# Byte offsets of the split weight slots in a decoder layer with a PEER expert network

## The chip, the cores and the metric

The kernel runs on one core of a Trainium2 chip. The metric is the device time of one execution in microseconds; the number compared is the median of several runs. One execution was also taken by the hardware profiler, and every row quoted here is from that one.

## What is computed

One layer on 256 tokens of 2048 float32 values. A projection feeds two mixers (a gated depthwise convolution with a layer norm, and a short gated convolution); their outputs go through a second projection and a layer norm. Then comes a PEER block: each token picks, for 8 heads, 16 of 16384 experts.

```
h  = x @ w_in + b_in
a  = silu(layer_norm(causal_conv31(a_val * sigmoid(a_gate))))
s  = sc_b * causal_conv3(sc_c * sc_h)
x1 = layer_norm(alpha * x + concat(a, s) @ w_out + b_out)
q  = x1 @ w_q;  scores against sub_keys;  top 16 of the sums -> experts, softmax g
act  = gelu(x1 . peer_u[experts]);  coef = act * g
x2 = layer_norm(alpha * x1 + sum(coef * peer_v[experts]))
```

## The kernel before, in words

The kernel does not gather the experts' rows of `peer_u`: it multiplies all of `peer_u` with x1, applies gelu, multiplies with a mostly zero matrix of gates, and multiplies the result with `peer_v`. For half of the columns of the second token block (`picked`) it gathers rows of `peer_v` instead, with POOL's indirect DMAs, and VectorE adds them up.

Float32 products are made from split numbers. Each number is written as hi + lo, both in the format float32r, and a product is three matmuls: hi by hi, hi by lo, lo by hi. The weights stream in as 656 units of 128 x 1024 float32 (512 KB), numbered `u`: 80 of `w_in`, 32 of `w_out`, 32 of `w_q`, 256 of `peer_u` ("up") and 256 of `peer_v` ("down"). For each unit:

- SP's queue loads it into a slot of `raw` (4 slots; in the down stage also 3 of `raw_late`), once the split of the unit that was there is done (`load`, L467).
- ACT copies it into `w_hi[u % 4]` (function `hi`, L627), once TensorE has used that slot's unit of four before (`used`).
- DVE subtracts, `w_lo[u % 4] = raw - w_hi` (function `lo`, L843); for the units of `w_q` and the first 36 of `peer_u` POOL does it instead (L571).
- PE waits for `lo_done` and runs its matmuls.

There are two kinds of unit on PE. For `w_in`, `w_q` and `peer_u` (368 units, function `stationary_unit`, L1411 to L1413) the weights are the stationary operand, 128 columns at a time, and the split x (`xt_hi`, `xt_lo`, 128 x 16 x 256) is the moving one, 256 columns: 24 matmuls a unit, 16 of them on `w_hi` and 8 on `w_lo`. For `w_out` (`out_units`, L1460 to L1462, split activations `mix_hi`, `mix_lo`) and `peer_v` (`down`, L1587 to L1589, split coefficients `c0` to `c4`) the roles are exchanged: 128 columns of activations or coefficients are stationary and 512 columns of weights move. The last four units of all do not go to `w_hi` and `w_lo` but to eight buffers of their own, `tail_hi0` to `tail_lo3`, and are read twice, once for each block of 128 tokens.

Between the up units, 32 batches of 8 short matmuls (L1553) build the gates from one-hot tables `oh1` (bfloat16) and `oh2g` (float16), 256 moving columns each.

SBUF is laid out by the order of the calls of `sb`, with some regions stacked on one another (`down0`, `down1`, `down2`, `early`, `route`). Each tensor takes its bytes per partition, rounded up to a multiple of 32. So the distance between two tensors follows from the sizes between them: from the end of `w_lo3` to the first of the split coefficients lie `stats` (192 bytes), `mv` (32), `rstd` (32) and `neg_mean` (32), together 288. All of `xt_hi`, `xt_lo`, `mix_hi`, `mix_lo`, the coefficient sets, `oh1`, `oh2g`, `raw_late`, `rows` and the `tail` buffers follow it at multiples of 128 bytes from each other; each slot of `w_hi` and `w_lo` starts at a multiple of 128 bytes from `raw`. The second family therefore stands 288 - 256 = 32 bytes off the first, counted modulo 128 (and modulo 64). The rows within a tensor step by 512, 1024 or 2048 bytes and change nothing in this.

```
mm(dst, hi_w[:, sl], xt_hi[:, kk, :], start=st, stop=False)
mm(dst, hi_w[:, sl], xt_lo[:, kk, :], start=False, stop=False)
i = mm(dst, lo_w[:, sl], xt_hi[:, kk, :], start=False, stop=en)
```

Of the kernel before, what the change touches and what calls it, by code (L numbers as in the profile page):

```python
# [5 lines left out]
P = 128  # L6
# [4 lines left out]
HALF = KT // 2  # L11
# [38 lines left out]
SPLIT = 4  # L50
# [116 lines left out]
def build(nc, x_t, x_nat, w_in, w_out, w_q, u_w, v_w, params, sub_keys, b_out, ln1_g, ln1_b, ln2_g, ln2_b, out):  # L167
    f32 = mybir.dt.float32
    f32r = mybir.dt.float32r
# [9 lines left out]
    with ctx:  # L179
        def sb(name, shape, dt, where=ctx):  # L180
            return where.enter_context(nc.sbuf_tensor(name, shape, dt))
# [2 lines left out]
            return ctx.enter_context(nc.semaphore(name))  # L184

        raw = sb("raw", [P, RAW, HALF * P], f32)
        w_hi = [sb(f"w_hi{i}", [P, HALF * P], f32r) for i in range(SPLIT)]
        w_lo = [sb(f"w_lo{i}", [P, HALF * P], f32r) for i in range(SPLIT)]
        stats = sb("stats", [P, TB, NCH, 6], f32)
        mv = sb("mv", [P, TB, 2], f32)  # L190
        rstd = sb("rstd", [P, TB, 1], f32)
        neg_mean = sb("neg_mean", [P, TB, 1], f32)

        def coefs(name, where):
            return [sb(f"{name}_{part}", [P, GROUP, T], f32r, where) for part in ("hi", "lo")]
# [1492 lines left out]
```

## Time and profile before

| | |
|---|---|
| median of 3 runs | 1747.68 us (1747.27 to 1749.12) |
| span of the profiled execution, first to last instruction | 1745.8 us |
| PE busy | 1713.3 us, 98% of the span |
| DVE busy | 1407.6 us, 81% |
| ACT busy | 854.0 us, 49% |
| POOL busy | 540.4 us, 31% |
| HBM traffic | 327 GB/s over the span |

The profiled execution's own time is given as its span; the median lies 1.9 us above it, which is work around the first and the last instruction. Busy time of PE counts a stretch as busy as long as some matmul is in flight; the matmuls overlap, so it does not tell whether they follow each other as closely as they could. That is read from the distance between the starts of neighbouring matmuls.

### The profile page before, as it was taken

To read this page: it belongs to the slowest core of one execution; us is meant where nothing else is said; L and a number is where in the kernel's file an instruction comes from. 1 tells how busy PE (TensorE), PEld (TensorE's weight loads), DVE (VectorE), ACT (ScalarE), POOL (GpSimd) and SP (SyncE) were. 2 spreads that over 40 slices of the span, in tenths; PEclk is the share of its full clock that TensorE was granted. 3 is DMA by queue.
4 is the path that set the end of the run, shared out by engine and by line. 5 is a ranking of instruction groups with operands and counts; after the bars stand their busy time and mean duration, and the time that the engine had idled before them with its cause. 6 is when DMAs were issued, how large, how long until landed. Compare 5 with 4: busy or idle time off the path is not lost.

```text
span 1745.8 us, 31461 instructions
## 1 busy us (share of the span) xinstructions
PE 1713.3 (98%) x11910; PEld 1578.1 (90%) x11910; DVE 1407.6 (81%) x1998; ACT 854.0 (49%) x1084; POOL 540.4 (31%) x342
## 2 busy tenths in 40 slices
PE   8999999899999999999999999999999999999997
PEld 8999987799999999999999999998788777878776
DVE  7999997678967677777777777556899898999997
ACT  5544436344544444444444444445555555555544
POOL 0000000288881000000000000004787777777731
PEclk9999999999999999999999999999999999999999
DMA  7787787777777777777677777899899999999994
GB/s 267 267 276 267 234 260 249 273 237 235 250 249 252 238 236 244 247 235 239 237 241 239 236 244 243 282 355 332 314 400 400 399 401 389 400 399 395 369 398 133
DMA packets 173728, 504.52 MB, mean 289 GB/s; under 512 B 19408, under 2 KB 35920, under 8 KB 172624
## 3 DMA queue, kind: packets, MB, share of 16 engines
q1 hardware_dynamic: 134000, 427.08, 70.0%
q0 software_dynamic: 22528, 67.19, 10.0%
q10 hardware_dynamic: 17120, 9.35, 1.8%
q8 instruction: 29, 0.48, 0.1%
q14 instruction: 51, 0.42, 0.1%
HBM read 490.98 MB, written 79.69 MB: 327 GB/s over the span
## 4 chain that ended last, share of the span: by engine, by line
PE 78%; DMA 6%; DVE 6%; issue 5%; POOL 3%; ACT 1%; DVEq 1%; SPq 0%; POOLq 0%; ACTq 0%
PE psum L1411 18%; PE psum L1413 18%; PE psum L1412 18%; PE psum L1587 6%; PE psum L1589 6%; PE psum L1588 6%; POOL sp_coef L588 2%; DVE w_lo L843 2%; DMA raw<-in_v_w_dram 2%; PE psum L1553 2%; DMA raw_late<-in_v_w_dram 1%; PE psum L1460 1%; PE psum L1462 1%; PE psum L1461 1%; DVE psum L1312 1%
## 5 line engine op out<-in xcount | busy, mean ns | idle before, releaser
L627 ACT ACTIVATE w_hi<-raw 128x1024 fp32r<-128x1024 f32 x547 | 578.9, 1060 | 682.1 <-PE psum L1413 487.1
L1411 PE MATMUL psum<-xt_hi,w_hi 128*128 128x256 f32 x2944 | 827.2, 281 | 5.3 <-DVE xt_lo L857 3.1
L1412 PE MATMUL psum<-xt_lo,w_hi 128*128 128x256 f32 x2944 | 822.6, 279 | 0.0
L1413 PE MATMUL psum<-xt_hi,w_lo 128*128 128x256 f32 x2944 | 822.4, 279 | 0.0
L843 DVE TENSOR_TENSOR w_lo<-raw,w_hi 128x1024 fp32r<-128x1024 f32 x479 | 581.8, 1222 | 221.5 <-ACT w_hi L627 219.7
L1411 PEld LDWEIGHTS psum<-xt_hi,w_hi 128*128 128x128 f32 x2944 | 554.3, 188 | 6.6 <-issue 6.0
L1412 PEld LDWEIGHTS psum<-xt_lo,w_hi 128*128 128x128 f32 x2944 | 554.3, 188 | 0.0
L1413 PEld LDWEIGHTS psum<-xt_hi,w_lo 128*128 128x128 f32 x2944 | 554.1, 188 | 0.0
L582 POOL DMA_INDIRECT rows<-v_rows,sp_idx x96 | 130.9, 1364 | 709.7 <-issue 674.9
L1587 PE MATMUL psum<-w_hi,c_hi 128*128 128x512 f32 x752 | 299.7, 399 | 8.9 <-DVE w_lo L843 8.7
L1589 PE MATMUL psum<-w_hi,c_lo 128*128 128x512 f32 x752 | 298.2, 396 | 0.0
L1588 PE MATMUL psum<-w_lo,c_hi 128*128 128x512 f32 x752 | 297.9, 396 | 0.0
L571 POOL TENSOR_TENSOR w_lo<-raw,w_hi 128x1024 fp32r<-128x1024 f32 x68 | 164.7, 2427 | 364.3 <-ACT w_hi L627 364.2
L588 POOL DMA_INDIRECT sp_coef<-hid_spill,sp_idx x128 | 193.0, 1508 | 55.2 <-issue 45.9
L1587 PEld LDWEIGHTS psum<-w_hi,c_hi 128*128 128x128 f32 x752 | 141.7, 188 | 49.5 <-DVE w_lo L843 15.4
L1589 PEld LDWEIGHTS psum<-w_hi,c_lo 128*128 128x128 f32 x752 | 141.6, 188 | 34.3
L1588 PEld LDWEIGHTS psum<-w_lo,c_hi 128*128 128x128 f32 x752 | 141.7, 188 | 33.3
L627 ACT ACTIVATE w_hi<-raw_late 128x1024 fp32r<-128x1024 f32 x105 | 111.3, 1060 | 103.2 <-PE psum L1589 75.0
L843 DVE TENSOR_TENSOR w_lo<-raw_late,w_hi 128x1024 fp32r<-128x1024 f32 x105 | 126.6, 1221 | 8.4 <-ACT w_hi L627 8.4
L1312 DVE SCALAR_TENSOR_TENSOR psum<-rows,sp_coef,psum 128x1024 f32<-128x1024 f32 x95 | 121.8, 1282 | 3.2 <-DMA rows<-v_rows,sp_idx 2.3
L882 DVE SCALAR_TENSOR_TENSOR cacc<-apad,prm,cacc x232 | 101.3, 480 | 0.0
L1293 DVE TENSOR_TENSOR c_lo<-hid,c_hi 128x1024 fp32r<-128x1024 f32 x32 | 39.2, 1224 | 22.9 <-ACT c_hi L776 22.8
(164 smaller groups left out, 1131.8 us busy)
## 6 DMA issues: line engine op xcount, KB each, us to landing
raw<-in_u_w_dram SPq DMA_DIRECT2D x256, 512.0 KB, 4.2
raw<-in_v_w_dram SPq DMA_DIRECT2D x148, 512.0 KB, 8.7
v_rows<-in_v_w_dram SPq DMA_DIRECT2D x128, 512.0 KB, 5.2
raw_late<-in_v_w_dram SPq DMA_DIRECT2D x108, 512.0 KB, 8.9
raw<-in_w_in_dram SPq DMA_DIRECT2D x80, 512.0 KB, 4.3
raw<-in_w_out_dram SPq DMA_DIRECT2D x32, 512.0 KB, 4.5
raw<-in_w_q_dram SPq DMA_DIRECT2D x32, 512.0 KB, 4.5
hid_spill<-hid ACTq DMA_DIRECT2D x7, 1024.0 KB, 15.4
```

The lines of the kernel that those rows point to most:

```text
L571: nc.gpsimd.tensor_tensor(w_lo[s][:, :], raw[:, s, :], w_hi[s][:, :].bitcast(f32), ALU.subtract).then_inc(lo_done[s], SPLIT)
L582: nc.gpsimd.indirect_dma_start(rows[k % ROWS][:, :], None, v_rows, bass.IndirectOffsetOnAxis(sp_idx[:, 1, k:k + 1], 0)).then_inc(rows_in[k ...
L588: nc.gpsimd.indirect_dma_start(sp_coef[:, k:k + 1], None, hid_dram, bass.IndirectOffsetOnAxis(sp_idx[:, 0, k:k + 1], 0)).then_inc(act_in[k ...
L627: nc.scalar.activation(parts_of(slot_u)[0][:, :], raw_of(slot_u), ACT.Copy).then_inc(hi_done, 1)
L843: tt(lo_w[:, :], raw_of(slot_u), hi_w[:, :].bitcast(f32), ALU.subtract).then_inc(lo_done[slot_u % SPLIT], SPLIT)
L1312: i = stt(picked[:, :], rows[k % ROWS][:, :], sp_coef[:, k:k + 1], picked[:, :], ALU.mult, ALU.add)
L1411: mm(dst, hi_w[:, sl], xt_hi[:, kk, :], start=st, stop=False)
L1412: mm(dst, hi_w[:, sl], xt_lo[:, kk, :], start=False, stop=False)
L1413: i = mm(dst, lo_w[:, sl], xt_hi[:, kk, :], start=False, stop=en)
L1587: mm(v_bank(j, b), c1, w1, start=st, stop=False)
L1588: mm(v_bank(j, b), c1, w2, start=False, stop=False)
L1589: i = mm(v_bank(j, b), c2, w1, start=False, stop=en)
```

## The change

The four slots of `w_hi` become slices of one tensor that is 6 elements longer, and start 0, 2, 4 and 6 elements (0, 8, 16, 24 bytes) behind a multiple of 4096 bytes. The four slots of `w_lo` become slices of one tensor that is 24 elements longer, and start 4, 8, 16 and 24 elements (16, 32, 64, 96 bytes) behind it. A tensor `place_pad` of 96 bytes that nothing uses is put in front of the coefficients. The number and order of the instructions on every engine, their shapes, waits and DMAs stay as they were; only addresses differ.

```
-        w_hi = [sb(f"w_hi{i}", [P, HALF * P], f32r) for i in range(SPLIT)]
-        w_lo = [sb(f"w_lo{i}", [P, HALF * P], f32r) for i in range(SPLIT)]
+        def placed(name, steps):
+
+            whole = sb(name, [P, SPLIT * HALF * P + steps[-1]], f32r)
+            return [whole[:, i * HALF * P + step:(i + 1) * HALF * P + step] for i, step in enumerate(steps)]
+
+        w_hi = placed("w_hi", [0, 2, 4, 6])
+        w_lo = placed("w_lo", [4, 8, 16, 24])
         stats = sb("stats", [P, TB, NCH, 6], f32)
         mv = sb("mv", [P, TB, 2], f32)
         rstd = sb("rstd", [P, TB, 1], f32)
         neg_mean = sb("neg_mean", [P, TB, 1], f32)
+        sb("place_pad", [P, 24], f32)
```

Rounded up to 32, the new `w_hi` is 32 bytes longer than the four old ones, the new `w_lo` 96 bytes, and the pad adds 96: from `w_hi0` on, the second family moves by 224 bytes, and its offset becomes 32 + 224 = 256, that is 0 modulo 128. Against it the weight slots stand so:

| slot | 0 | 1 | 2 | 3 |
|---|---|---|---|---|
| `w_hi`, bytes | 0 | 8 | 16 | 24 |
| `w_lo`, bytes | 48 | 64 | 96 | 128 |

(`w_lo` has 32 bytes more than its steps because it starts 32 bytes later behind the longer `w_hi`.) The `tail` buffers keep an offset of 0 against the coefficients, as before. `raw` stays where it was; `raw_late`, `rows` and `row_late`, which DMAs fill, move with the second family.

## Rows read from the trace of the kernel before

**Rows 1.** The page: busy time by engine, and the 40 slices.
```profile
PE 1713.3 (98%) x11910; PEld 1578.1 (90%) x11910; DVE 1407.6 (81%) x1998; ACT 854.0 (49%) x1084; POOL 540.4 (31%) x342
PEclk9999999999999999999999999999999999999999
```

**Rows 2.** Stages by window: PE, PEld, DVE, ACT, POOL busy, clock, DMA share, GB/s.
```profile
0.00:1184.00 1184.00, 1170.52 (x9607) 1145.95 (x9608) 905.23 (x1535) 552.93 (x788) 166.44 (x80) 1.00 0.75 253
1184.00:1716.00 532.00, 523.13 (x2220) 416.39 (x2220) 482.94 (x431) 292.94 (x283) 366.34 (x256) 1.00 1.00 381
```

**Rows 3.** Timeline of PE in the up stage, first and 148th of a run.
```profile
1109.98 0.28 PE L1411 MATMUL psum<-xt_hi,w_hi 128*128 128x256 f32 x1
...
1127.13 0.28 PE L1411 MATMUL psum<-xt_hi,w_hi 128*128 128x256 f32 x1
```

**Rows 4.** Timeline of PE in the down stage, first and 73rd of a run.
```profile
1561.67 0.40 PE L1587 MATMUL psum<-w_hi,c_hi 128*128 128x512 f32 x1
...
1578.47 0.40 PE L1587 MATMUL psum<-w_hi,c_hi 128*128 128x512 f32 x1
```

**Rows 5.** Timeline of PE, first pass over the tail units; 12 matmuls lie between the rows.
```profile
1719.20 0.39 PE L1588 MATMUL psum<-tail_lo,c_hi 128*128 128x512 f32 x1
...
1721.92 0.39 PE L1588 MATMUL psum<-tail_lo,c_hi 128*128 128x512 f32 x1
```

**Rows 6.** Timeline of PE, second pass: the first tail matmul, the sixth, the eighth, the last.
```profile
1730.02 0.39 PE L1587 MATMUL psum<-tail_hi,c_hi 128*128 128x512 f32 x1
...
1731.17 0.39 PE L1589 MATMUL psum<-tail_hi,c_lo 128*128 128x512 f32 x1
...
1731.63 0.39 PE L1588 MATMUL psum<-tail_lo,c_hi 128*128 128x512 f32 x1
...
1735.25 0.39 PE L1589 MATMUL psum<-tail_hi,c_lo 128*128 128x512 f32 x1
```

**Rows 7.** Timeline of PE, one batch of gates: start, time, and x8 merged.
```profile
700.67 1.08 PE L1553 MATMUL psum<-oh2g,oh 128*128 128x256 f16 x8
```

**Rows 8.** PE's groups by line and shape: count, busy us, mean ns, idle before.
```profile
L1411 PE MATMUL psum<-xt_hi,w_hi 128*128 128x256 f32 x2944 | 827.2, 281 | 5.3 <-DVE xt_lo L857 3.1 <-issue 2.3
L1587 PE MATMUL psum<-w_hi,c_hi 128*128 128x512 f32 x752 | 299.7, 399 | 8.9 <-DVE w_lo L843 8.7
L1460 PE MATMUL psum<-w_hi,mix_hi 128*128 128x512 f32 x128 | 51.0, 399 | 1.9 <-DVE mix_lo L997 1.1 <-DVE lnt L1024 0.8
```

**Rows 9.** DMA in 40 slices of 1200 to 1700 us, and its sum.
```profile
GB/s 401 234 285 277 403 398 402 400 400 400 399 398 403 399 399 399 403 400 400 399 378 383 401 399 401 402 400 402 390 403 402 380 401 392 343 350 408 410 408 400
DMA packets 58255, 193.15 MB, mean 386 GB/s; under 512 B 10119, under 2 KB 10123, under 8 KB 58238
```

**Rows 10.** DVE's and ACT's splits by line: min/median/max ns.
```profile
L843 DVE TENSOR_TENSOR w_lo<-raw,w_hi x479: 1202/1224/1298, 5.2 to 1715.4; 128x1024 fp32r<-128x1024 f32 x160
L843 DVE TENSOR_TENSOR w_lo<-raw_late,w_hi x105: 1205/1217/1273, 1195.4 to 1712.0; 128x1024 fp32r<-128x1024 f32 x105
L627 ACT ACTIVATE w_hi<-raw x547: 1041/1062/1071, 4.0 to 1713.2; 128x1024 fp32r<-128x1024 f32 x183
L627 ACT ACTIVATE tail_hi<-raw_late x3: 1041/1043/1062, 1715.1 to 1717.6; 128x1024 fp32r<-128x1024 f32 x3
```

**Rows 11.** The convolution's taps on DVE, one line: min/median/max ns.
```profile
L882 DVE SCALAR_TENSOR_TENSOR cacc<-apad,prm,cacc x232: 471/479/492, 26.3 to 251.1; - x116
```

**Rows 12.** DMA issues of 1200 to 1700 us: KB each, median us to landing.
```profile
raw<-in_v_w_dram SPq DMA_DIRECT2D x132, 512.0 KB, 8.8
raw_late<-in_v_w_dram SPq DMA_DIRECT2D x100, 512.0 KB, 9.0
```

## The prediction

> **What bounds the kernel now.** I read the page first: PE is busy 98% of the span at full granted clock [rows 1], so the time is PE's, and the question is whether its matmuls follow each other as closely as they can. The stages split it in two [rows 2]. Up to 1184 us PE is busy 1170.5 us with DVE at 905 and ACT at 553 us: what a matmul gets cheaper there comes off the end. From 1184 to 1716 us PE still has 523 of 532 us, but DVE has 483 and the DMA engines are full, at 390 GB/s or more in 32 of 40 slices [rows 9]; a faster PE would soon wait there.
>
> Then the timeline, for the distance between starts. In the up stage 147 matmuls take 1127.13 - 1109.98 = 17.15 us, 116.67 ns each for 256 columns [rows 3]. In the down stage 72 take 16.80 us, 233.33 ns each for 512 columns [rows 4]. The tail units run the same instruction on the same coefficients, only on weights in other buffers: 12 matmuls in 2.72 us, 226.67 ns each [rows 5], and again 3.62 us for 16 in the second pass [rows 6]. That is 6.67 ns or 2.9% less, while ACT and DVE were still at work in the first of these passes. By the layout, the difference is this: `w_hi` and `w_lo` stand 32 bytes (modulo 64) off the coefficients, the tail buffers 0. A gate matmul has 256 columns and two operands at offset 0 to each other: (1.08 - 0.28) / 7 = 114 ns [rows 7], where the same offset 0 should give 116.67 x 226.67 / 233.33 = 113.33. So I read the trace as: **the offset between the two operands of a matmul costs up to 3.33 ns of 116.67, or 6.67 of 233.33**, and all weight slots pay the whole of it today.
>
> The Trainium skill's page "TensorE: Matmul & The Clock Gate", section "Back-to-back issue gap", gives N / 2.4 + 2.5 ns for a warm matmul, 109.2 ns at 256 columns and 215.8 at 512. The trace does not agree: 116.67 and 233.33, and the tail's 226.67 is above it too. By the page up to 8832 x 7.5 = 66 us would be there to gain; my sum goes by the rows and has less than half of that.
>
> **The change part by part.** No instruction, wait or DMA is added, removed or reordered. Only addresses move, so each term is a duration that may change.
>
> *Full prize.* Weights stationary: 3 x 2944 = 8832 matmuls [rows 8] x 3.33 ns = 29.4 us. `w_out`: 3 x 128 = 384 x 6.67 = 2.6 us. Down: 3 x 752 = 2256 x 6.67 = 15.0 us. Together 47 us, if every slot came to the tail's rate. The tail's own 48 matmuls keep offset 0: nothing.
>
> *How much each slot gets.* Two points are measured: offset 0 gives all, 32 gives none. Offsets 64 and 128 I take as 0, and 96 as 32 (the present weights are 32 below the coefficients, thus 96 modulo 128, and pay in full in both roles). For 8, 16, 24 and 48 nothing is measured; the bounds are all and none, and I take the share in proportion to the distance from the measured points. `w_hi` (offsets 0, 8, 16, 24): 1, 0.75, 0.5, 0.25, mean 0.625. `w_lo` (48, 64, 96, 128): 0.5, 1, 0, 1, mean 0.625. So 0.625 whatever the weight of hi and lo.
>
> *Changing offsets.* Now hi and lo matmuls of a unit have different offsets, two by one in turn, which no stretch of the trace has. Nearest are the two entries into the tail units, where the offset changes once. The first runs at 226.67 at once; in the second, the first five matmuls take 1.15 us, 230 ns each [rows 6], half of the gain. The mean of both is 0.75. Bounds: 0 (the gain never settles) and 1. So 0.625 x 0.75 = 0.47 of the prize.
>
> - Stationary stages: 29.4 x 0.47 = 13.8 us, on the path.
> - `w_out`: 2.6 x 0.47 = 1.2 us.
> - Down: 15.0 x 0.47 = 7.1 us on PE. DMA moves 193 MB in 500 us at 386 GB/s against a plateau of 400 to 403 [rows 9], so it could give some 3.5% at the utmost, and the low slices come early, while PE waits for gathers and the spill. DVE has 483 of 532 us. I take a third, 2.3 us; bounds 0 and 7.1.
>
> *ACT and DVE on the moved slots.* ACT's split writes 1041 to 1071 ns wherever source and target lie; DVE's 1202 to 1298 [rows 10], with medians of 1224 and 1217 for sources 32 bytes apart. Offsets that are no multiple of 32 are shown only by reads: the taps read `apad` at every step of 4 bytes and stay within 471 to 492 ns [rows 11]. Writes at 8, 16 or 24 bytes have no row. I cost them at nothing; up to 1184 us DVE's idle time covers them. Where that cover is thin, in the down stage, 2% on 256 splits (24 ns each) would be 6 us of DVE, of which perhaps half shows. Bound: +3 us. Against it, `raw_late` lands in 9.0 us and `raw` in 8.8 [rows 12], and `raw_late` now gets `raw`'s alignment: 0 to 3 us in a stage that waits for DMA. I leave both at zero.
>
> Sum: 13.8 + 1.2 + 2.3 = 17.3 us. Against the profiled span, 1745.8 - 17.3 = 1728.5; the median of the runs is 1.9 us above the span, which gives 1730.4. I say **1730 us**. Its own range is 1722 to 1740.
>
> **The rivals.**
>
> *Only the aligned slots gain, or all but one.* If the offset must be exactly a multiple of 64, `w_hi0`, `w_lo1` and `w_lo3` gain: 1/4 of 2/3 and 2/4 of 1/3, together 1/3 of the matmuls, 9.8 + 0.9 + 1.7 = 12 us at most: 1735, inside the range of the forecast. If only 32 and 96 are bad, 11/12 gain: 27 + 2.4 + 5 = 34 us, 1713. For that speaks that the cost is exactly the same in both roles, like a collision at one place; against it, that 32 would have to be the one bad spot. Chance 0.1.
>
> *The offset is not what made the tail fast.* The tail buffers also lie elsewhere, 100 KB up, near the coefficients they meet, and `oh1` and `oh2g` are neighbours as well. If the place and not the offset counts, nothing moves: 1747.7. The Trainium skill, "SBUF — State Buffer", section "Who interferes with whom", speaks for this outcome: PE has two read ports of its own that are independent, and only the pair that DVE and GpSimd share is contended. By that rule the offset would change nothing; the step from 233.33 to 226.67 shows that something about the place matters, so I give it no more than 0.15.
>
> *Offsets inside 32 bytes cost, slower.* Every operand of PE in this trace starts at a multiple of 32. A stream that starts 8, 16, 24 or 48 bytes off such a line may need one fetch more per piece than it does now. Price: as much again as the present 32 bytes cost, 3.33 ns a matmul (6.67 at 512 columns). It hits three of four hi slots and one of four lo slots, 1/2 + 1/12 = 7/12 of the matmuls, while 1/3 gain; net 1/4 of the prize is lost: 29.4 / 4 + 17.6 / 4 = 11.8 us, 1759.5. It decides from the point where the misaligned slots cost more than 3.33 x (1/3) / (7/12) = 1.9 ns a matmul. The rows say nothing against it. Nearly the same comes out if it is the absolute start that counts, and starting at a multiple of 64 (as the weights do now, and x and the coefficients will) is what is slow. Chance 0.2. The same skill page speaks of 16-byte lines, where each crossing to a new one costs something; no row here shows it on PE.
>
> **How the numbers follow.** Forecast, a partial gain: 0.55. Nearly all gain: 0.1. Nothing: 0.15. Slower: 0.2. A measurement of this kernel can tell about 0.2%, 3.5 us, from no change. The first case reaches within 3.5 us of 1747.7 with about 0.03 of its chance. So faster 0.62, same 0.17, slower 0.21. The range goes from 1715, which leaves out half of the nearly-all case, to 1757, which takes in nothing and the milder half of the slower case: about 0.15 lies outside.
>
> **What would show it.** In the timeline of PE, eight different stretches instead of one: units with slot 0 nearer 113.33 ns a matmul, slots 1, 2 and 3 less so in this order, the lo matmuls of slots 1 and 3 fast and that of slot 2 still at 116.67. If all units stay at 116.67, the second rival holds. If slots 1 to 3 are above 116.67, the third does. The down stage should keep its 400 GB/s with more waits of ACT for `raw`; if its length falls by more than 7 us, DMA was not its bound. DVE's and ACT's splits should keep 1224 and 1062 ns; if they grow at slots 1 to 3, the writes cost. The prediction is wrong if the time before 1184 us does not fall by 8 to 20 us.

## The result, and the profile after

| | before | after |
|---|---|---|
| median, 4 runs each | 1747.47 us | 1762.55 us |
| ratio of the times | | 1.0082 (95%: 1.0065 to 1.0100) |
| span of the profiled execution | 1745.8 us | 1760.5 us |
| start of the first down matmul | 1183.8 us | 1197.7 us |
| from there to the start of the last matmul | 551.4 us | 552.2 us |

The change makes the kernel 0.8% slower. Of the 14.7 us, 13.9 lie before the first matmul of the down stage.

The page and the stage windows (columns as in [rows 1, 2]):

```profile
PE 1726.9 (98%) x11910; PEld 1595.2 (91%) x11910; DVE 1402.7 (80%) x1998; ACT 854.6 (49%) x1084; POOL 519.3 (29%) x342
PEclk9999999899999999999999999999999999999999
```
```profile
0.00:1197.00 1197.00, 1184.59 (x9601) 1159.99 (x9602) 900.06 (x1535) 553.71 (x788) 151.55 (x80) 1.00 0.76 250
1197.00:1729.00 532.00, 521.06 (x2221) 418.25 (x2220) 481.66 (x431) 291.27 (x282) 360.06 (x256) 0.99 1.00 381
```

In the first window PE is busy 14.1 us longer, for the same matmuls; ACT stayed within 1 us, DVE and POOL got less busy. In the second window PE's busy time changed by 2 us, and the DMA share, the GB/s and the length not at all. The timeline of PE after, 192 matmuls (eight units) of the up stage apart, and 72 of the down stage:

```profile
1129.76 0.28 PE L1419 MATMUL psum<-xt_hi,w_lo 128*128 128x256 f32 x1
...
1152.49 0.28 PE L1419 MATMUL psum<-xt_hi,w_lo 128*128 128x256 f32 x1
```
```profile
1299.62 0.40 PE L1593 MATMUL psum<-w_hi,c_hi 128*128 128x512 f32 x1
...
1316.34 0.40 PE L1593 MATMUL psum<-w_hi,c_hi 128*128 128x512 f32 x1
```

22.73 us / 192 = 118.39 ns against 116.67 in [rows 3], and 16.72 / 72 = 232.2 against 233.33 in [rows 4]. Below, "pitch" is the mean distance between the starts of neighbouring matmuls over the whole trace. Only distances under 150 ns (up, q and w_in units, "up ns" in the table) or under 270 ns (down) are counted; the longer ones are waits or other work. Before it was 116.66 and 233.2 ns, after it is 118.25 and 232.2. The product 8832 x (118.25 - 116.66) = 14.0 us is the whole loss before the down stage. The tail units, whose distance is the same as before, still come to 226.67 ns ((1749.87 - 1747.15) / 12), though only after some ten matmuls of each pass:

```profile
1747.15 0.39 PE L1595 MATMUL psum<-tail_hi,c_lo 128*128 128x512 f32 x1
...
1749.87 0.39 PE L1595 MATMUL psum<-tail_hi,c_lo 128*128 128x512 f32 x1
```

The splits, min/median/max ns, and the landings from 1200 to 1700 us:

```profile
L849 DVE TENSOR_TENSOR w_lo<-raw,w_hi x479: 1205/1224/1280, 5.2 to 1729.9; 128x1024 fp32r<-128x1024 f32 x160
L849 DVE TENSOR_TENSOR w_lo<-raw_late,w_hi x105: 1205/1217/1271, 1209.1 to 1726.6; 128x1024 fp32r<-128x1024 f32 x105
```
```profile
L633 ACT ACTIVATE w_hi<-raw x547: 1041/1062/1073, 4.0 to 1727.7; 128x1024 fp32r<-128x1024 f32 x183
```
```profile
raw<-in_v_w_dram SPq DMA_DIRECT2D x134, 512.0 KB, 8.0
raw_late<-in_v_w_dram SPq DMA_DIRECT2D x102, 512.0 KB, 8.3
```

DVE's and ACT's medians for the slots are those of [rows 10] to the nanosecond, though ACT's targets now start at 8, 16 and 24 bytes and DVE's at 16 bytes in one slot: these writes cost nothing. `raw_late` still lands 0.3 us after `raw`. So the loss is PE's own, in the 256-column matmuls.

### The profile page after: what moved, and what is told of

It reads as the page before. It is cut to its first block, busy times and chain, and to the rows that moved or that the text cites. A ratio compares the mean times of both kernels' runs of the same rounds, so it can differ in the third digit from the quotient of the medians.

```text
span 1760.5 us, 31461 instructions
## 1 busy us (share of the span) xinstructions
PE 1726.9 (98%) x11910; PEld 1595.2 (91%) x11910; DVE 1402.7 (80%) x1998; ACT 854.6 (49%) x1084; POOL 519.3 (29%) x342
## 4 chain that ended last, share of the span: by engine, by line
PE 87%; DMA 4%; DVE 4%; issue 2%; ACT 1%; POOL 1%; DVEq 0%; SPq 0%; POOLq 0%; ACTq 0%
PE psum L1417 20%; PE psum L1418 20%; PE psum L1419 20%; PE psum L1593 7%; PE psum L1594 7%; PE psum L1595 7%; DMA raw<-in_v_w_dram 3%; DVE w_lo L849 2%; PE psum L1559 2%; PE psum L1466 1%; PE psum L1467 1%; PE psum L1468 1%; DVE psum L1318 1%; ACT w_hi L633 1%; DMA raw_late<-in_v_w_dram 1%
## 5 line engine op out<-in xcount | busy, mean ns | idle before, releaser
L849 DVE TENSOR_TENSOR w_lo<-raw,w_hi 128x1024 fp32r<-128x1024 f32 x479 | 582.1, 1223 | 229.0 <-ACT w_hi L633 227.5
L577 POOL TENSOR_TENSOR w_lo<-raw,w_hi 128x1024 fp32r<-128x1024 f32 x68 | 149.8, 2206 | 383.7 <-ACT w_hi L633 383.7
L594 POOL DMA_INDIRECT sp_coef<-hid_spill,sp_idx x128 | 184.5, 1442 | 55.5 <-issue 46.3
```

Source lines behind the costliest of these rows:

```text
L577: nc.gpsimd.tensor_tensor(w_lo[s][:, :], raw[:, s, :], w_hi[s][:, :].bitcast(f32), ALU.subtract).then_inc(lo_done[s], SPLIT)
L594: nc.gpsimd.indirect_dma_start(sp_coef[:, k:k + 1], None, hid_dram, bass.IndirectOffsetOnAxis(sp_idx[:, 0, k:k + 1], 0)).then_inc(act_in[k ...
L849: tt(lo_w[:, :], raw_of(slot_u), hi_w[:, :].bitcast(f32), ALU.subtract).then_inc(lo_done[slot_u % SPLIT], SPLIT)
```

## The experiments

The distance of a slot is the start of x (or of the coefficients) less the start of the slot, in bytes modulo 256; why 256 is shown in the second group. Before, all eight slots had distance 32. The change gives `w_hi` 0, -8, -16, -24 and `w_lo` -48, -64, -96, -128 (in the expectations "below x" sometimes stands for the size alone). The kernels differ from the one before only in this layout, made so:

```
+        steps = [0, 0, 0, 0, 16, 16, 16, 16]
+        whole = sb("w_parts", [P, 2 * SPLIT * HALF * P + steps[-1]], f32r)
+        places = [whole[:, i * HALF * P + step:(i + 1) * HALF * P + step] for i, step in enumerate(steps)]
+        w_hi, w_lo = places[:SPLIT], places[SPLIT:]
         ...
+        sb("place_pad", [P, 8], f32)
```

with other `steps` and another pad. Where x had to come nearer, `stats`, `mv`, `rstd` and `neg_mean` moved behind `sp_tok`. "Before" is the old kernel on the same chip. The times of the change, u0, u0at32, u8, h0l64 and h128l64 are medians of 4 to 10 executions, all others are of one. On one chip the old kernel alone went from 1746.3 to 1755.8 us in 11 executions, so a single time tells no difference of a few us; the pitch is the finer measure (u0, u0at32 and d128, of equal distance, agree to 0.02 ns in the up column).

| kernel | distance hi / lo | up ns | down ns | us | before, us |
|---|---|---|---|---|---|
| before | 32 / 32 | 116.66 | 233.2 | | 1747.5 |
| the change | 0..-24 / -48..-128 | 118.25 | 232.2 | 1762.6 | 1747.5 |
| u0 | 128 / 128 | 119.67 | 232.7 | 1770.1 | 1751.4 |
| u0at32 | 128 / 128 | 119.68 | 232.7 | 1775.2 | 1751.4 |
| u8 | 120 / 120 | 118.03 | 233.3 | 1755.4 | 1751.4 |
| h0l64 | 128 / 64 | 115.65 | 231.1 | 1733.5 | 1751.4 |
| d0 | 0 / 0 | 119.93 | 227.2 | 1776.2 | 1750.5 |
| d256 | 0 / 0 | 119.92 | 227.2 | 1776.7 | 1750.5 |
| d128 | 128 / 128 | 119.66 | 232.7 | 1774.3 | 1750.5 |
| d64 | 64 / 64 | 117.78 | 233.3 | 1759.1 | 1750.5 |
| whole32 | 0 / -32..-128 | 118.67 | 231.5 | 1766.2 | 1748.8 |
| steps32 | 32..8 / -16..-96 | 118.69 | 231.3 | 1766.3 | 1748.8 |
| h32lm32 | 32 / -32 | 117.78 | 233.2 | 1757.9 | 1748.8 |
| h128l0 | 128 / 0 | 118.34 | 229.0 | 1751.7 | 1748.8 |
| pairs | 32, 24, 16, 8, hi = lo | 118.06 | 233.0 | 1763.0 | 1746.9 |
| lomix | 32 / -16..-96 | 118.54 | 232.6 | 1762.2 | 1746.9 |
| h160l96 | 160 / 96 | 118.05 | 233.0 | 1762.5 | 1746.9 |
| h96l32 | 96 / 32 | 120.00 | 235.2 | 1777.5 | 1746.9 |
| u24 | 24 / 24 | 118.09 | 233.7 | 1764.9 | 1750.2 |
| h128l64 | 128 / 64 | 115.93 | 231.1 | 1736.2 | 1750.2 |

**All slots alike, or hi and lo apart.** u0: steps 0, pad 24 elements, so x is 384 past. u0at32: steps 8, pad 24 + 8 for the same distance from other absolute starts. u8: steps 2. h0l64: the diff above.

> All eight weight slots at offset 0 against x and the coefficients, at multiples of 128 bytes. Theory A (each matmul is slowed by its own offset; 0 is fast, as in the tail units): 113.33 ns a matmul with 256 columns, the time before 1184 us falls by 25 to 29 us, about 1715 us. Theory B (what slows is that neighbouring matmuls have different offsets; a common offset of any size is fast): the same. Theory C (not the offset but the place of the buffers): 116.67 ns and 1747 us. Theory D (starting at a multiple of 64 is slow): slower than before, 120 ns.

> All eight slots and x and the coefficients 32 bytes past a multiple of 128: offset 0 again, other absolute starts (those of the tail units). Theories A and B: the same time as all slots at offset 0 at multiples of 128. Theory D (absolute starts count, multiples of 64 slow): faster than that one by 10 us or more.

> All eight slots at offset 8 bytes. Theory A with a cost inside 32 bytes (the slower rival): 118 to 120 ns a matmul, 1765 us or more. Theory A with a cost in proportion to the offset: 114.2 ns, about 1722 us. Theory B (only changing offsets cost): near 113.33 ns or a constant near it, about 1715 to 1720 us.

> w_hi at offset 0, w_lo at offset 64: no offset inside 32 bytes, but hi and lo differ. Theory A (own offset modulo 64): as all slots at 0, about 1715 us. Theory B (changing offsets cost): slower than that, 116 to 119 ns a matmul, 1745 to 1770 us.

The first and the 193rd matmul of the same stretch of the up stage, in u0 and in h0l64:

```profile
1129.82 0.29 PE L1416 MATMUL psum<-xt_hi,w_parts 128*128 128x256 f32 x1
...
1152.86 0.29 PE L1416 MATMUL psum<-xt_hi,w_parts 128*128 128x256 f32 x1
```
```profile
1129.81 0.28 PE L1416 MATMUL psum<-xt_hi,w_parts 128*128 128x256 f32 x1
...
1152.00 0.28 PE L1416 MATMUL psum<-xt_hi,w_parts 128*128 128x256 f32 x1
```

120.00 and 115.57 ns. Theory A and B both said that u0 would be the fast one; its time is 1.0105 of the kernel before (1.0088 to 1.0122), more than the change's 1.0082. Theory D alone had foreseen u0's 120 ns, but u0at32 has the same pitch to 0.02 ns from other absolute starts, so D falls: the relation between the operands is what counts. C falls too, since the weight slots stayed where they were and the pitch moved. u8 is 8 bytes off a multiple of 32 and faster than u0, which is not (u8's time is 1.0027 of the kernel before, 1.0017 to 1.0036). h0l64 is faster than the kernel before, 0.9911 (0.9886 to 0.9937), and its 1733.5 us lie between what A and B had foreseen.

**Which modulus, and does the distance 0 help.** Steps 0; the small tensors moved to the end; pads of 0, 16, 32 and 64 elements.

> The small tensors between weights and coefficients are moved to the end, so the distance from the end of w_lo to the coefficients is 0, and x and the coefficients stand 0 modulo 512 from all eight slots. Theory E (the distance counts modulo 512 or more, and 0 there is what makes the tail fast): 226.67 ns in the down stage, 113.33 ns in the up stage, about 1715 us. Theory F (only the distance modulo 128 counts): as the kernel with all slots at 0 and distance 384, 119.67 ns and 232.7 ns, about 1768 us.

> Distance 64 bytes, all slots alike. Theory F with period 64: 119.67 ns in the up stage. Theory F with period 128, or theory E: another value, between 113 and 119 ns; 1715 to 1760 us.

> Distance 128 bytes, all slots alike. Theory F: 119.67 ns and 232.7 ns exactly, about 1768 us. Theory E: some other value.

> Distance 256 bytes, all slots alike. Theory F: 119.67 ns and 232.7 ns exactly, about 1768 us. Theory E with period 256: as distance 0; with period 512 or more: some other value.

Timeline of d0, 192 matmuls of the up stage apart and 72 of the down stage apart:

```profile
1129.82 0.28 PE L1412 MATMUL psum<-xt_lo,w_hi 128*128 128x256 f32 x1
...
1152.86 0.28 PE L1412 MATMUL psum<-xt_lo,w_hi 128*128 128x256 f32 x1
```
```profile
1534.79 0.39 PE L1589 MATMUL psum<-w_hi,c_lo 128*128 128x512 f32 x1
...
1551.11 0.39 PE L1589 MATMUL psum<-w_hi,c_lo 128*128 128x512 f32 x1
```

120.00 and 226.67 ns, the tail's own value; over the whole down stage the pitch is 227.2. d0 and d256 agree to 0.01 ns in the up stage and to 0.1 in the down stage, d128 and u0 (384) as well, and d0 and d128 differ by 5.5 ns in the down stage (only by 0.3 in the up stage): theory F falls, and the distance counts modulo 256. Its effect need not be the same in the two roles: distance 0 makes the 512-column matmuls nearly as fast as the tail (theory E, right), and the 256-column ones 3.3 ns slower than before (E, wrong). (Elsewhere the roles agree: 96 / 32 is the slowest in both, 128 / 64 below the old pitch in both.) The gain in the down stage brings no time: d0's down stage is 553.3 us against 551.4 before, although the pitch saves 2255 x 6.09 ns = 13.7 us (233.31 and 227.22 ns without the tail). What the longer distances (270 ns and more) hold above the pitch grows from 19.8 to 35.4 us, 15.6 us more, and so ACT's waits for `raw` and `raw_late` to land, from 62.5 to 85.2 us in the windows of that stage. The window of d0's down stage:

```profile
1211.00:1740.00 529.00, 510.50 (x2201) 414.22 (x2200) 478.22 (x427) 289.05 (x279) 368.83 (x256) 0.99 1.00 381
```

PE is busy 510.5 of 529 us there, against 523.1 of 532 in [rows 2], with DMA still at a share of 1.00 and 381 GB/s.

One thing in the traces goes with the layout and is not PE's. In the slices of 1300 to 1700 us the median DMA rate is 399 to 400 GB/s in 14 of the 20 kernels and 410 to 413 in the other six: u0, u8, h0l64, d128, h128l0 and h128l64. These six, and no others, have the coefficients, `raw_late` and `rows` (which DMAs fill) 128 bytes behind a multiple of 256, counted from `raw`; u0at32, on u0's chip, has them at 160 and 400 GB/s. Slices of d0 and of h0l64:

```profile
GB/s 406 401 400 399 401 402 399 398 401 388 392 400 396 403 400 400 400 400 384 366 356 407 399 401 400 400 400 402 384 400 399 401 398 401 400 395 350 352 407 409
```
```profile
GB/s 409 400 416 414 414 412 415 413 413 413 415 413 414 413 410 409 395 413 413 417 406 409 378 393 389 412 408 364 375 374 366 388 415 414 419 419 418 410 212 234
```

In the 14 kernels the down stage takes 550.1 to 555.1 us whether the pitch is 227.2 or 235.2 ns; in the six it takes 542.2 to 550.4. So at the lower rate the stage goes by DMA and not by the pitch, and at the higher one it is shorter. Which of the moved tensors brings the higher rate, no run separates.

**What in the change costs.** whole32: its steps rounded to multiples of 32 (hi 0; lo 32, 64, 96, 128 bytes). steps32: the change's steps, x 32 bytes further. h32lm32 and h128l0: all four slots alike, `w_lo` 64 or 128 bytes past `w_hi`'s grid.

> The change with every offset a multiple of 32: x 0 modulo 256 from w_hi in all four slots, w_lo 32, 64, 96 and 128 below x. Theory G (the distance modulo 256 counts, and 0 is the worst place for 256-column matmuls, 120.0 ns): as slow as the change or slower, 118 to 119.5 ns, 1762 us or more. Theory H (the offsets inside 32 bytes are what costs): faster than the change by 10 us or more.

> The steps of the change with x and the coefficients 32 bytes past it, the distance that the kernel before had: hi slots 32, 24, 16 and 8 below x, lo slots -16, -32, -64, -96. Theory G (uniform slots at 32 gave 116.67, at 0 gave 120.0): between these, 116.7 to 118.2 ns, 1748 to 1760 us. Theory H (offsets inside 32 bytes cost): no better than the change, 118.2 ns or more, 1762 us.

> w_hi 32 below x (as before), w_lo 64 bytes further on, 32 above x, all four slots alike. If hi and lo 64 bytes apart is what helped in the kernel with 128 and 64 (115.65 ns): 113.3 to 115.7 ns and 1725 to 1735 us. If only each slot's own distance counts: at least 116.67 ns and 1747 us or more.

> w_hi 128 below x, w_lo 0, all four slots alike. If each matmul had the price of its own distance (119.7 at 128, 120.0 at 0): 119.8 ns, 1770 us. If the change between hi and lo matters: below 117 ns.

Timeline of whole32 and of steps32, 192 matmuls of the up stage apart:

```profile
1129.78 0.28 PE L1414 MATMUL psum<-xt_hi,w_parts 128*128 128x256 f32 x1
...
1152.57 0.28 PE L1414 MATMUL psum<-xt_hi,w_parts 128*128 128x256 f32 x1
```
```profile
1129.77 0.28 PE L1414 MATMUL psum<-xt_hi,w_parts 128*128 128x256 f32 x1
...
1152.61 0.28 PE L1414 MATMUL psum<-xt_hi,w_parts 128*128 128x256 f32 x1
```

118.70 and 118.96 ns. Without any offset inside 32 bytes the kernel (whole32) is as slow as the change: theory H falls. With x brought back to its old distance (steps32) it does not get better, where theory G wanted a value between those of 32 and 0, at most 118.2: G falls as well, though it named whole32 rightly. h32lm32 (117.78) shows that 64 bytes between hi and lo are no gain by themselves, and h128l0 (118.34) is faster than both of its distances alone (119.67 and 119.93), though not below 117 as the other expectation had it: a matmul does not simply pay the price of its own distance.

**Mixtures.** pairs: steps 0, 0, 2, 2, 4, 4, 6, 6 with `w_hi, w_lo = places[0::2], places[1::2]`. lomix: hi 0; lo 12, 16, 24, 32 elements. Both leave `w_hi0` at the old distance. h160l96 and h96l32: h0l64 with x 32 bytes further or nearer. u24: all slots at 24.

> Hi and lo of a slot have the same distance to x (32, 24, 16, 8 bytes for slots 0 to 3), so the distance changes only from unit to unit. Theory J (a mixture of distances keeps the two streams from settling and costs about 118.5 ns wherever it lies): 118 to 118.8 ns, 1760 to 1768 us. If each unit pays the price of its own distance (116.67 at 32 to 120.0 at 0): 117 to 119.2 ns with a clear rise from slot 0 to slot 3. If only differences within a unit cost: 116.7 ns.

> w_hi as before (32 below x in all slots), w_lo with the spread of the change (-16, -32, -64, -96). Theory J: 118 to 118.8 ns, 1760 to 1768 us. If the spread of w_hi is what costs: near 117 ns, 1750 us.

> All eight slots at distance 24 bytes, the distance at which slot 1 of the kernel with pairs ran at 120.0 ns. Theory K (a unit pays the price of its own distance, and the price is a rugged function of it): 119.5 to 120.5 ns, about 1775 us. Theory J (the slots' mixture is what made slot 1 slow): between the uniform values at 0 (119.9) and 32 (116.67) and not above 119 ns.

> All slots alike, w_hi 160 and w_lo 96 below x: as the fast kernel (128 and 64) but 32 bytes on. If the gain belongs to hi and lo 64 bytes apart around the opposite end of the 256 bytes: 115 to 116.5 ns and 1728 to 1745 us. If it is a narrow spot: 117.5 ns or more.

> All slots alike, w_hi 96 and w_lo 32 below x: the fast kernel 32 bytes the other way. The same alternatives: 115 to 116.5 ns and 1728 to 1745 us, or 117.5 ns and more.

Both mixtures cost 1.4 and 1.9 ns, as theory J said: a change from unit to unit is enough, and one of `w_lo` alone is too. By slot, from the starts in the up units after the last gates: pairs has 117.35, 120.04, 118.73 and 117.48 ns for distances 32, 24, 16 and 8, no rise from slot 0 to slot 3. A rugged price of single distances (theory K) could have explained slot 1, but all slots at 24 run at 118.09 (118.33 in those last units): K falls, J's bound of 119 holds. The change has 118.64, 117.69, 118.57 and 118.61 there. The two neighbours of the fast arrangement, 32 bytes on either side, are at 118.05 and 120.00: it is a narrow spot. The six single distances measured (0, 24, 32, 64, 120, 128) have a mean of 118.4 ns, and the mixtures lie around it. This fits a reading in which the steps add no cost of their own kind but take the kernel from the best of these single values to about their mean; no run proves it.

**The fast arrangement again.** h128l64: steps as in h0l64, small tensors at the end, pad 16 elements.

> The fast arrangement once more, w_hi 128 and w_lo 64 bytes below x in all slots, but with the small tensors moved to the end, so that the distance is less by 256 bytes. If only the distance modulo 256 counts: 115.65 ns in the up stage, 231.1 ns in the down stage, and 0.991 of the time of the kernel before. Otherwise another value.

231.1 ns in the down stage as expected and 115.93 in the up column, 0.3 more than the other layout with the same distances. The rest lies mostly in one stage: in the `w_in` units the pitch is 116.70 here and 115.56 in h0l64, in the last up units 115.56 in both. So the modulus of 256 holds in the up units, and the same distances can run at two pitches. The time is 0.9919 of the kernel before (0.9898 to 0.9940). Both kernels with 128 and 64 beat both kernels of this case: 8832 x 0.7 to 1.0 ns = 6.4 to 8.9 us come from the stationary units, the rest from `w_out` and the down stage. That stage takes 542.2 and 549.1 us in the two against 551.4 before, and both have the higher DMA rate, so what it gives is not the gain of the pitch alone.

## Why the prediction was wrong

- **"Offset 0 gives all, 32 gives none".** This is the step that failed: the cost of an offset. It was read in the down stage and the tail, where the weights move in 512 columns, and carried over to the stationary units, where x moves in 256 columns and where 29.4 of the 47 us prize lay. (Whether the role or the number of columns makes the difference, no run separates.) There, of the six distances measured with all slots alike (0, 24, 32, 64, 120, 128), 0 is the worst (119.9 ns) and 32 the best (116.66). For its own role the step was right: d0 gives 227.2 ns.
- **The gate matmul as a witness, 113.33 ns for 256 columns.** It misled: split weights at distance 0 run at 119.9 to 120.0. The gate matmul has 16-bit operands [rows 7]; that this is why it differs is not tested.
- **Modulo 64.** Wrong, it is 256: in the down stage 64 and 128 give 233.3 and 232.7 ns, 0 gives 227.2.
- **0.625 by distance, and 0.75 for changing offsets.** Both were shares of a gain that did not exist here. The five kernels with unlike slots come out at 118.1 to 118.7 ns, against 116.66 a loss.
- **13.8 us gained in the stationary stages.** It was 14.0 us lost. `w_out` gained 384 x 1.0 ns = 0.4 us instead of 1.2.
- **Down: 7.1 us on PE of which a third shows.** The pitch gained 1.0 ns, 2.3 us in all, and none of it shows. That DMA is the bound there was right, and d0 shows it more sharply than the change. That its rate itself can depend on the layout (400 or 412 GB/s) was not foreseen.
- **ACT and DVE at nothing.** Right: the medians did not move.
- **The rivals.** The slower one foresaw 1759.5 and the result was 1762.6, but by a mechanism that the runs speak against: whole32 is as slow without a single offset inside 32 bytes, and u8 and u24, with all slots 8 bytes off, are faster than u0 and d0. That the place of the tail made it fast, with no effect of the offset, was refuted by d0, whose ordinary slots reach the tail's 226.67 ns; so was, for this kernel, the independence of PE's two reading streams that the Trainium skill's page "SBUF — State Buffer" states in "Who interferes with whom". Moving the operands against each other changes the pitch from 115.65 to 120.00 ns with only addresses changed.
- The signs to look for were named rightly (time before the down stage, pitch by slot, unchanged splits), and the first of them says at once that the forecast failed.

## What to carry to other kernels

Read the distance between starts, not the busy share: PE was 98% busy before, after and in d0, h0l64 and h96l32, while its rate in the up stage varied by 4% among them with the addresses of its operands. A layout effect that is read in one role (which operand moves, how many columns, what type) is to be measured again in the other before it is priced. A regular layout may sit on a good spot by luck; keep the slots of a ring alike and scan the distance between stationary and moving operands in steps of 32 bytes over 256, with hi and lo apart as a second axis. Alike alone is no gain: at 0 and at 128 it was slower than every mixture.

## What the runs showed of the hardware

- With matmuls back to back at a granted clock of 0.99 to 1.00 (the 2.4 GHz level), the pitch depends on the distance between the stationary and the moving tensor modulo 256 bytes: float32r, 256 columns, 115.65 to 120.00 ns; 512 columns, 227.2 to 235.2 ns. A shift of all operands by 32 bytes changes nothing (u0 and u0at32, 119.67 and 119.68 ns).
- The distance does not settle the pitch alone. With all slots alike, u0, u0at32 and d128 run at 118.67 ns in the `w_in` units and at 120.00 in the last up units, u24 at 117.78 and 118.33, h128l64 at 116.70 and 115.56; the kernel before keeps 116.67 throughout.
- At distance 0 the two kinds differ by 227.2 - 119.9 = 107.3 ns for 256 more columns, so 119.9 - 107.3 = 12.6 ns of the shorter one are not in proportion to its columns; at distance 32 the pitch is in proportion to the columns (116.66, 233.2).
- A unit's pitch depends on its neighbours: with distance 24, 120.04 ns between other distances (pairs) and 118.33 among its like (u24), both in the last up units.
- The median DMA rate in the down stage was 410 to 413 GB/s in the six kernels whose later DMA targets start 128 bytes behind a multiple of 256 from `raw`, and 399 to 400 in the other 14. Nothing was run to test this by itself.
- Unlooked for, POOL's subtraction of 128 x 1024 takes 17% less time when `w_hi` starts 8 or 24 bytes off a multiple of 32 from `raw`: 2005 and 2006 ns in u8 and u24, where all slots are 8 off. In u0 and whole32, where every start is a multiple of 32, it is 2417, near the 2427 before. The change has a mean of 2206, and by slot medians of 2399, 2000, 2404 and 2001 ns for `w_hi` at 0, 8, 16 and 24 bytes. DVE's and ACT's splits show nothing of the kind, and no time came of it, since POOL waits for ACT there. Groups of POOL before, in the change, and in u8:

```profile
L571 POOL TENSOR_TENSOR w_lo<-raw,w_hi 128x1024 fp32r<-128x1024 f32 x68 | 164.7, 2427 | 364.3 <-ACT w_hi L627 364.2
```
```profile
L577 POOL TENSOR_TENSOR w_lo<-raw,w_hi 128x1024 fp32r<-128x1024 f32 x68 | 149.8, 2206 | 383.7 <-ACT w_hi L633 383.7
```
```profile
L574 POOL TENSOR_TENSOR w_parts<-raw,w_parts 128x1024 fp32r<-128x1024 f32 x68 | 136.1, 2005 | 397.0 <-ACT w_parts L630 397.0
```
- What mechanism makes the pitch was not found. No theory here foretells the pitch of a new pair of distances; the table is a map of 16 sets of distances, in 20 kernels, and no more.
